# One 512-column matmul for both halves of the activations, and VectorE adds the halves

## What is computed

```python
for i in range(DEPTH):                       # kinds: a, b, c, a
    xn = rms_norm(h, norm_gain[i])
    m = mixer(xn, ...)                       # a: diff_attention, b: mla, c: rglru_block
    h = h + m                                # m ends in  y @ w_out
    g = sigmoid(rms_norm(h, ple_norm[i]) @ ple_w_gate[i])
    h = h + g * (p[i] @ ple_w_proj[i])
...
# second block: layer 0 is an SSD mixer ("s"), layer 1 dilated attention ("d")
x = layer_norm(DEEPNORM_ALPHA * x + (1.0 + gate) * y, ln_g[layer], ln_b[layer])
```

## Time and profile before

| what | value |
|---|---|
| median of 3 runs | 4247.78 us (4247.11 to 4262.5) |
| profiled execution, first to last instruction | 4257.0 us |
| mean granted TensorE clock in it | 0.950 of full speed |
| TensorE busy | 3822.6 us, 90% |
| VectorE busy | 2778.6 us, 65% |
| ScalarE busy | 2089.6 us, 49% |
| GpSimd busy | 599.0 us, 14% |

### The profile page before, as it was taken

One profiled execution on the slowest core, in us unless ns is written; L12 is line 12 of the kernel. 1 busy time (PEld: TensorE's weight loads), 2 busy tenths in 40 slices (PEclk: granted clock), 3 DMA queues, 4 the chain that ended last, 5 costly groups with the idle time before them and its releaser, 6 DMA issues.

```text
span 4257.0 us, 80674 instructions
## 1 busy us (share of the span) xinstructions
PE 3822.6 (90%) x29682; PEld 3641.7 (86%) x29682; DVE 2778.6 (65%) x4250; ACT 2089.6 (49%) x3218; POOL 599.0 (14%) x564
## 2 busy tenths in 40 slices
PE   7999998988889886798999989889999897899997
PEld 6898888877779886798989889788989886799996
DVE  6676665566666675566667666678787774754555
ACT  5555544555545546555555544444454443443442
POOL 1011012100002201122101111223121221100000
PEclk9999999999999987899999999899999998899998
DMA  5555544444444432344555444343434342244442
GB/s 211 188 206 190 187 169 155 162 178 169 176 152 176 150 139 100 141 168 159 198 187 198 186 161 178 138 149 138 160 136 157 143 151 95 109 168 160 161 167 89
DMA packets 93571, 681.56 MB, mean 160 GB/s; under 512 B 10401, under 2 KB 10529, under 8 KB 11169
## 3 DMA queue, kind: packets, MB, share of 16 engines
q1 hardware_dynamic: 92880, 676.75, 43.6%
q0 software_dynamic: 464, 1.64, 0.1%
HBM read 676.25 MB, written 2.10 MB: 159 GB/s over the span
## 4 chain that ended last, share of the span: by engine, by line
PE 60%; DVE 15%; issue 10%; ACT 9%; POOL 4%; DVEq 1%; ACTq 0%; DMA 0%; POOLq 0%; SPq 0%
PE g L336 18%; PE g L337 17%; PE g L338 17%; DVE w_lo L1263 5%; ACT w_hi L789 4%; POOL scratch L2052 3%; PE norm_bank L349 1%; PE g L396 1%; PE g L395 1%; DVE scratch L1759 1%; ACT scratch L829 1%; ACT scratch L828 1%; PE turn_bank L375 1%; DVE scratch L1325 1%; PE g L408 1%
## 5 line engine op out<-in xcount | busy, mean ns | idle before, releaser
L1263 DVE TENSOR_TENSOR w_lo<-w_raw,w_hi 128x1024 fp32r<-128x1024 f32 x1280 | 1578.8, 1238 | 936.1 <-ACT w_hi L789 933.2
L789 ACT ACTIVATE w_hi<-w_raw 128x1024 fp32r<-128x1024 f32 x1280 | 1322.9, 1053 | 1328.4 <-PE g L338 1310.9
L336 PE MATMUL g<-p_hi,w_hi 128*128 128x256 f32 x4624 | 1346.8, 291 | 59.0 <-DVE scratch L1669 17.2
L337 PE MATMUL g<-p_lo,w_hi 128*128 128x256 f32 x4624 | 1324.3, 286 | 0.0
L338 PE MATMUL g<-p_hi,w_lo 128*128 128x256 f32 x4624 | 1323.5, 286 | 0.0
L336 PE MATMUL g<-q_hi,w_hi 128*128 128x256 f32 x3472 | 1004.5, 289 | 51.4 <-DVE q_lo L1833 14.8
L337 PE MATMUL g<-q_lo,w_hi 128*128 128x256 f32 x3472 | 991.4, 286 | 0.0
L338 PE MATMUL g<-q_hi,w_lo 128*128 128x256 f32 x3472 | 991.3, 285 | 0.0
L336 PEld LDWEIGHTS g<-p_hi,w_hi 128*128 128x128 f32 x4624 | 902.1, 195 | 74.3 <-DVE w_lo L1263 39.8
L337 PEld LDWEIGHTS g<-p_lo,w_hi 128*128 128x128 f32 x4624 | 903.4, 195 | 1.0
L338 PEld LDWEIGHTS g<-p_hi,w_lo 128*128 128x128 f32 x4624 | 902.8, 195 | 0.0
(11 more groups left out here) (339 smaller groups left out, 3750.8 us busy)
## 6 DMA issues: line engine op xcount, KB each, us to landing
w_raw<-in_slots SPq DMA_DIRECT2D x640, 1024.0 KB, 4.8
h<-in_x SPq DMA_DIRECT2D x1, 2048.0 KB, 10.9
out_h<-h SPq DMA_DIRECT2D x1, 2048.0 KB, 6.3
scratch<-in_p POOLq DMA_DIRECT2D x4, 256.0 KB, 3.8
con<-in_consts SPq DMA_DIRECT2D x1, 878.0 KB, 4.9
scratch<-in_distance POOLq DMA_DIRECT2D x1, 576.0 KB, 4.0
vec<-in_vecs SPq DMA_DIRECT2D x1, 383.0 KB, 3.2
scratch<-in_positions SPq DMA_DIRECT2D x1, 128.0 KB, 6.5
```

What stands on the lines that cost most here:

```text
L336: pe.matmul(g, wh, hi[:, k], start=n == 0, stop=False)
L337: pe.matmul(g, wh, lo[:, k], start=False, stop=False)
L789: act.activation(w_hi[k % SPLIT][:, cols], raw[k % RAW][:, cols], ACT.Copy).then_inc(hi_ready, 1)
L1263: dve.tensor_tensor(w_lo[k % SPLIT][:, cols], raw[k % RAW][:, cols], w_hi[k % SPLIT][:, cols], SUB).then_inc(lo_ready, 1)
```

## The change

The high and the low part of an activation tile now lie side by side (`p_both`, `q_both`, 512 numbers a row). In `square_tiles` the block `w_hi` takes both in one matmul of 512 columns, whose result fills the whole bank, high part in the left half and low part in the right; `w_lo` still takes the 256 columns of the high part, into the left half. VectorE's new `join` reads the 512 columns and adds right to left; where something is to be done to the sum, a second instruction does it, after a wait for VectorE's own semaphore `dve_step`. A table of counts for the loops (`PER_LOOP`) follows from that.

```diff
-    p_hi, p_lo = sb("p_hi", [P, DT, SEQ], F32R), sb("p_lo", [P, DT, SEQ], F32R)
-    q_hi, q_lo = sb("q_hi", [P, DT, SEQ], F32R), sb("q_lo", [P, DT, SEQ], F32R)
+    p_both, q_both = sb("p_both", [P, DT, 2, SEQ], F32R), sb("q_both", [P, DT, 2, SEQ], F32R)
+    p_hi, p_lo, q_hi, q_lo = [x[:, :, n] for x in (p_both, q_both) for n in range(2)]
...
         def square_tiles(hi, lo, arriving=0):

             w = slot()
-            tile(w, range(SLOT), hi, lo, range(SLOT), arriving=arriving)
+            both = p_both if hi is p_hi else q_both
+            pe.wait_ge(tile_taken, c.at("tile", -1))
+            g = G[c.bank]
+            c.bank ^= 1
+            for k in range(SLOT):
...
+                wh, wl = w_hi[w][:, k * P:(k + 1) * P], w_lo[w][:, k * P:(k + 1) * P]
+                x = both[:, k].rearrange("p a b -> p (a b)")
+                if k == 0:
+                    pe.matmul(g[:], wh, x, start=True, stop=False)
+                last = pe.matmul(g[:, 0:SEQ], wl, hi[:, k], start=False, stop=False)
+                if k:
+                    last = pe.matmul(g[:], wh, x, start=False, stop=k == SLOT - 1)
...
+        def join(dst):
+
+            dve.wait_ge(tile_done, c.next("tile"))
+            g = G[c.bank].rearrange("p (a b) -> p b a", a=2)
+            c.bank ^= 1
+            return dve.tensor_reduce(dst, g, AX.X, ADD)
...
                     for j in range(4):
                         begin()
-                        g = take()
-                        dve.tensor_tensor(zg[:, j % 2], g, rstd[:], MUL).then_inc(tile_taken, 1)
+                        link(join(zg[:, j % 2]))
+                        dve.tensor_tensor(zg[:, j % 2], zg[:, j % 2], rstd[:], MUL).then_inc(tile_taken, 1)
                         lo_half(1)
...
-                    g = take()
-                    dve.tensor_tensor(h[:, n], g, h[:, n], ADD).then_inc(tile_taken, 1)
+                    link(join(sg[:, j % 2]))
+                    dve.tensor_tensor(h[:, n], sg[:, j % 2], h[:, n], ADD).then_inc(tile_taken, 1)
...
-                dve.tensor_tensor(dst, g, rstd[:], MUL).then_inc(tile_taken, 1)
+                link(join(dst))
+                if first and j == 0:
+                    factor()
+                dve.tensor_tensor(dst, dst, rstd[:], MUL).then_inc(tile_taken, 1)
...
-                g = take()
-                dve.tensor_copy(dsts[n], g).then_inc(tile_taken, 1)
+                join(dsts[n]).then_inc(tile_taken, 1)
```

More of the change, by code:

```diff
@@ L116, in program @@
     with ctx:
-        _program(nc, ctx, t, counts)
+        _program(nc, ctx, t, PER_LOOP)
 def _program(nc, ctx, t, counts):
@@ L381, in square_tiles @@
             w = slot()
-            tile(w, range(SLOT), hi, lo, range(SLOT), arriving=arriving)
+            both = p_both if hi is p_hi else q_both
[3 more added lines that the diff above has]
+            for k in range(SLOT):
+                if k == SLOT // 2:
+                    second_half()
+                if arriving == DT or arriving == 1 and k in (0, SLOT - 2):
+                    pe.wait_ge(x_lo, c.next("x") if arriving == DT else c.at("x", -1 if k == 0 else 0))
+                wh, wl = w_hi[w][:, k * P:(k + 1) * P], w_lo[w][:, k * P:(k + 1) * P]
[5 more added lines that the diff above has]
+                    last = pe.matmul(g[:], wh, x, start=False, stop=k == SLOT - 1)
+                if k == SLOT // 2 - 1:
+                    last.then_inc(half_used, 1)
+            last.then_inc(tile_done, 1)
+            c.next("tile")
         def mod_slot(m, fresh=False):
@@ L1386, in a_head @@
                 begin()
-                g = take()
-                if first and j == 0:
-                    factor()
                 dve.wait_ge(scaled, c.at("scaled"))
@@ L1509, in b_pair @@
             begin()
-            g = take()
-            dve.tensor_tensor(b_gz[:, 0], g, rstd[:], MUL).then_inc(tile_taken, 1)
+            link(join(b_gz[:, 0]))
+            dve.tensor_tensor(b_gz[:, 0], b_gz[:, 0], rstd[:], MUL).then_inc(tile_taken, 1)
             lo_half(1)
@@ L1519, in b_pair @@
             begin()
-            g = take()
-            dve.tensor_tensor(b_gz[:, 1], g, rstd[:], MUL).then_inc(tile_taken, 1)
+            link(join(b_gz[:, 1]))
+            dve.tensor_tensor(b_gz[:, 1], b_gz[:, 1], rstd[:], MUL).then_inc(tile_taken, 1)
             mod_columns(i, 34)
@@ L1544, in layer_b @@
                 begin()
-                g = take()
+                link(join(b_cs[:, n % 2]))
                 if n == 0:
                     factor()
-                dve.tensor_tensor(b_cs[:, n % 2], g, rstd[:], MUL).then_inc(tile_taken, 1)
+                dve.tensor_tensor(b_cs[:, n % 2], b_cs[:, n % 2], rstd[:], MUL).then_inc(tile_taken, 1)
                 lo_half(1)
@@ L1620, in c_input @@
                 begin()
-                g = take()
                 xb = xbp[:, j % 2]
-                dve.tensor_tensor(xb[:, 3:259], g, rstd[:], MUL).then_inc(tile_taken, 1)
+                link(join(xb[:, 3:259]))
+                dve.tensor_tensor(xb[:, 3:259], xb[:, 3:259], rstd[:], MUL).then_inc(tile_taken, 1)
                 lo_half(1)
@@ L1667, in layer_c @@
                         begin()
-                        t_ = take()
-                        dve.tensor_tensor(c_gz[:, j % 2], t_, rstd[:], MUL).then_inc(tile_taken, 1)
+                        link(join(c_gz[:, j % 2]))
+                        dve.tensor_tensor(c_gz[:, j % 2], c_gz[:, j % 2], rstd[:], MUL).then_inc(tile_taken, 1)
                         lo_half(1)
@@ L1782, in s_group @@
                 begin()
-                g = take()
-                dve.tensor_copy(s_xbp[:, n % 2, 3:3 + SEQ] if n < 6 else s_z[:, n - 6], g).then_inc(tile_taken, 1)
+                join(s_xbp[:, n % 2, 3:3 + SEQ] if n < 6 else s_z[:, n - 6]).then_inc(tile_taken, 1)
                 lo_half(1)
@@ L1857, in layer_s @@
             begin()
-            g = take()
-            dve.tensor_scalar(s_dt[:], g, V("s_dt_bias"), None, ADD).then_inc(tile_taken, 1)
+            link(join(s_dt[:]))
+            dve.tensor_scalar(s_dt[:], s_dt[:], V("s_dt_bias"), None, ADD).then_inc(tile_taken, 1)
             lo_half(1)
```

37 lines of the change are left out of this document (added).

## The result

| | before | after |
|---|---|---|
| time of the runs, us | 4252.98 (4247.11 to 4262.5, 4 runs) | 4376.94 (4371.35 to 4383.86, 4 runs) |
| span of the profiled run, us | 4257.0 | 4382.1 |
| mean granted clock in it | 0.950 | 0.933 |

The ratio is 1.029, with a 95% interval of 1.027 to 1.031: the change costs 124 us. The forecast was 4288, slower, within 4205 to 4345. The sign was right and the size three times too small.

What follows compares the result with a forecast made beforehand. TensorE was taken to bound outs and d heads, VectorE's takes gates, layer c and a heads; -24.3 + 2.8 - 30.4 + 44 + 27 + 13 - 2 + 8 + 2 = +40, 4247.8 + 40 = 4288 us, range 4205 to 4345.

Steps and rivals of the forecast that it cites:

- The lower bound that I gave, 0.21: TensorE's square tiles: if 0.013 us stays on both matmuls, a block takes 0.347 and a tile saves 0.21 us.
- the second ("keeps the 0.013"): Rival on some 236 TensorE-paced tiles: the 512-column matmul keeps 0.013, 0.17 us less saved each, +40, 4328; chance 0.13.
- The rival of 1.2 us: VectorE's 512-column reduction takes 1.2 us: +105 us, 4393; chance 0.10 together with the clock.
- GpSimd's collision with the second instruction: VectorE's instruction after the reduction slowed beside GpSimd: +0.17 on 161 takes, +27, 4315; within the forecast's 0.44.
- Gates and layer c: VectorE's take is in the pacing loop, 0.71 us longer a turn: gates +44 us, layer c +13.
- The chain of takes: A heads: five takes add 3.55 us against 0.18 slack, four other tiles give -1.52; net +1.9 a head, +27 in all.
- The rival of slack in the chains: A heads absorb the 3.55 us in idle time and gain on all eight tiles: -49, 4212; chance 0.18.
- The rival of the clock: New stalls bring TensorE's clock down in the heads: +4.8 us a head, +77, 4365; chance 0.10 together with the reduction.
- The term of 1.04 us a pair: Layer b's 8 pairs: take +0.71 and first take's chain +0.33 delay mod_columns' small matmuls; +8 us.
- Outs: 64 tiles, TensorE-bound with room on VectorE: -24.3 us; the last tile's later take adds +2.8 at gates' starts.
- D heads: 80 tiles bound by TensorE, the join's +0.26 us beside 47% idle VectorE: -30.4 us.

Runs made afterwards that it cites:

- the join alone: Against the kernel before: three 256-column matmuls a block again, aimed at the bank's two halves, which VectorE joins; 4447.27 us, ratio 1.044.
- with the clock held and the collision gone: Changed kernel with 9 small matmuls ahead of mod_columns in each b pair and VectorE waiting for GpSimd's clamp before w_lo; 4355.2 us, one run.
- the executions with 366.7: Changed kernel with other block forms in the outs (4350.83 us), or w_lo's product in the bank's right half (4378.19 us); b pairs 366.7 and 366.8.
- the clamp first: Changed kernel, but in a b pair VectorE waits for GpSimd's clamp of the first gate tile before w_lo; 4363.94 us, ratio 1.024.

## Why the prediction was right and wrong

- **Pace of the 512-column matmul: wrong, and this is the step that failed.** I took 0.216 for it and left 0.120 for its neighbour, that is, I let the 0.013 us go from the wide one because float32 matmuls of the norms ran at 0.216. It stays (0.228 alone), and beside a narrow one there are 0.006 more: block 0.354 where I had 0.336, and 0.11 us a tile where I had 0.38. The reading of the norm rows was carried over to another kind of matmul, and that was wrong. The lower bound that I gave, 0.21, was not low enough, because I had not thought that the mixture could cost something. The prediction's own terms spend 0.38 on some 240 tiles, so the miss is 0.27 x 240 = 65 us. Of the rivals it is the second ("keeps the 0.013"), to which I gave 0.13, and which asked for 40 of them.
- **Join and second instruction: right.** 0.686 against 0.683, and 0.42 for the instruction behind it (1178.09 above). VectorE's busy time came out at 3003 us and not near 3090, a figure for which the prediction shows no sum. The rival of 1.2 us is out, and so is GpSimd's collision with the second instruction.
- **Gates and layer c: right.** 7.23 us a turn. The stretches that hold them missed by 5 to 12 us; at 0.27 a tile the outs in them make 4 to 9 of that.
- **A heads: mechanism right.** The chain of takes sets the head: 68.0 against 65.0, where 1.9 was forecast. With 0.11 for each of the four free tiles in place of 0.38 the same sum gives 3.55 - 0.18 - 0.44 = 2.9, and the head without half clock took 2.6 more. The rival of slack in the chains is out; the takes did push TensorE, by the pauses forecast, though ahead of `mod_columns` (1.83 us) and hardly of a tile (0.16). The rival of the clock was argued from a stall of 4.13 us, longer than the 1 to 2 us of my new ones. But in the trace of the kernel before 6.8 us of half clock already stood behind a pause of 1.84 us in two a heads. In the changed kernel this cost stayed about where it was (four heads longer by 1.1 to 3.0 us, against three by 1.7 to 3.0 before); with the join alone it came in twelve heads of fourteen.
- **B pairs: wrong in size.** The term of 1.04 us a pair holds: with the clock held and the collision gone the seven pairs are 7.5 us longer (one execution), and I had 7.3. What I missed are the other 25 us, or 17 by the executions with 366.7. The join fills a wait of VectorE that had kept `w_lo` clear of GpSimd's clamp, and the pause of 2.94 us which comes of both is followed by 10 to 17 us at half clock, over score products that nothing hides. I had looked for the clock in the a heads (0.10 with the reduction), where the slices of 3.4 us after the new pause cost at most 0.4 us a head. The Trainium skill's rule on "SBUF — State Buffer", section Who interferes with whom, which the prediction applied to the second instruction alone, agrees with the clamp's 0.85 and 1.68 us: it speaks of any VectorE instruction with two inputs in SBUF, and `w_lo` is one.
- **Outs: right but for the pace.** The joins are hidden, as the version with the new form in outs and d heads alone shows.
- **D heads: right by luck in part.** The stretch gained 16.9 us. At 0.11 us, 70 tiles make 8. The other 8 to 9 are two pauses of the kernel before, of 3.0 and 3.2 us with half clock behind the first, which stand 131 us apart at the turns of the loop over pairs of heads:

```profile
3902.49 0.58 PE L336 MATMUL g<-q_hi,w_hi 128*128 128x256 f32 x1 [2.99 <-DVE w_lo L1263]
```

They occur with three matmuls a block (the kernel before, and the join alone) and in none of the others, all of which took 433.0 us. Here the releaser named had been done for 0.96 us, and the wait behind it has no row. The packets of the instruction queue go with the pauses. In each of the four (two here, two in the join alone) a packet of 16 KB starts 0.3 to 0.5 us after TensorE has stopped, and TensorE goes on 2.6 to 2.7 us after that start. With three matmuls a block such packets come in every head of d, 4 to 6 each; in the other kernels, three a head at first and none in the last three heads of the stretch. So these pauses look like TensorE waiting for its program at the turn of a loop that is fetched anew each time. The packets don't say which engine they are for, and no run tested it.

Sum of the miss: +65 for the pace, +25 for the b pairs, -8 for the pauses in d, which makes 82 of 85 us.

The join alone had 200 us more at half clock than before, and cost 57 us more than the prediction's terms make without a faster TensorE (+40, and the 0.38 us on some 240 tiles taken out, +92: 132). The stretches say where 54 of them are: 31 us lie in the fourteen a heads, which grew by 78 where 3.55 - 0.18 each makes 47, and 23 in the b pairs (372.3 against 341.6, with 7.3 forecast). In the a heads it is the clock, by the twelve heads that took 71.2 to 71.8 us beside two of 68.0 and 68.6. In the b pairs it is the clock and the collision together.

What stays open: the 0.006 us of the mixed block; what the weight load has to do with the fixed 0.013; what in the two pauses of d TensorE waits for; and why one pause of 2 us in an a head is followed by half clock and the next is not.

## What to carry to other kernels

Fewer, wider instructions save only the fixed part of what they replace: here 0.013 us of 0.120, once a block, and half of it was lost again to the mixture. Measure the pace of the new form in its new neighbourhood before its saving is multiplied by thousands, and give its bound a side on which the saving is nearly nothing. Read a stretch in more than one execution: the same seven b pairs took 374.4, 366.7 and 366.8 us. When a change lengthens an instruction in a chain, ask for every wait that it fills what that wait had kept apart, and for every pause of TensorE that it makes what stands right behind the pause: if that is TensorE work which nothing hides, the pause is paid twice. And a change with a cost in chains and a gain in streams should be made in the streams only.

## What the runs showed of the hardware that was not expected

- A matmul of the fast kind (fp32r) here costs its columns at 2.4 GHz and 0.013 to 0.015 us more, at 256 and at 512 columns, whether the weights that are loaded for it are new or the same again. A 512-column one and a 256-column one in turn cost 0.353 to 0.354 together, not 0.347.
- A 128-column matmul between 256-column ones starts the next after 0.06 us, but itself starts 0.17 after them: the pair takes 0.23 us, where its columns need 0.16. The Trainium skill, "TensorE: Matmul & The Clock Gate", section Back-to-back issue gap, gives N/2.4 + 2.5 ns as the isolated gap of one warm matmul, 216 for 512 columns. The trace does not agree: this kernel's 512-column matmuls alone, each with a weight load of its own, ran at 228.
- Between the 17 runs of the kernel before that one comparison took, the time follows the mean clock: 4249.39 us at 0.952 and 4268.59 at 0.947, that is 19 us for some 43 us more at half clock. Two single runs of one kernel can so be 0.45% apart.
- A pause of 2.94 us in the b pairs was followed by 10 to 17 us at half clock in the changed kernel, one of 2.11 us by 7 to 10 us with the clamp first. With the pause filled, 14 to 38 us at half clock are left over all seven pairs, where 31 stood before the change. A pause of 1.8 to 2.1 us in the a heads was followed by 6.8 us at half clock in some heads and by none in others of the same kernel.
